# Expert weights of a mixture-of-experts kernel: which rows a partition takes

## The chip, the cores and the metric

The kernel runs on one core of a Trainium2 chip. Its time is the device time of one execution, in microseconds (us); it is given as the median of several runs. Beside the timed runs, one execution was recorded by the hardware profiler; its trace is what the views below are taken from.

## What is computed

One layer of a diffusion backbone over 128 context tokens and 256 latent tokens (T = 384), width D = 2048, in float32. The first half (modulation, input projection, attention and a short convolution, output projection) fills the first 700 us and is not touched by the change. The second half is a routed mixture of 16 experts with hidden width FF = 1024, of which each sees at most 48 tokens:

```
def ec_moe(h, w_router, w_gate, w_up, w_down):
    ...
    xs = jax.vmap(lambda hb, ib: hb[ib])(h, idx)
    a = jnp.einsum('becd,edf->becf', xs, w_gate)
    u = jnp.einsum('becd,edf->becf', xs, w_up)
    y = jnp.einsum('becf,efd->becd', jax.nn.silu(a) * u, w_down)
    y = y * gate[..., None].astype(y.dtype)
    ...
```

So each expert needs three matrices of 8 MiB: w_gate and w_up with 2048 rows of 1024 numbers (4 KB a row), w_down with 1024 rows of 2048 numbers (8 KB a row). All 16 experts together read 384 MiB (403 MB) of weights from HBM once.

## The kernel before

**Slots and order.** The experts are taken in eight pairs. A pair has six matrices in the order MATS: gate and up of expert 0, gate of expert 1, down of expert 0, up of expert 1, down of expert 1. Each matrix comes in four parts of 2 MiB, so a pair has 24 parts, q0 to q23: q0 to q3 gate 0, q4 to q7 up 0, q8 to q11 gate 1, q12 to q15 down 0, q16 to q19 up 1, q20 to q23 down 1. A part lies in one of the eight slots of the tile `ring`, 16 KB in each of the 128 partitions (the list ORDER says which part goes to which slot). SyncE (SP) issues one DMA per part (`expert_load`, L345 to L356): it waits on `moe_used` until the part that had the slot eight parts ago has been used, and then issues. The first eight loads wait for tiles of the first half that lie in the same memory. TensorE (PE) waits on `moe_landed` of the slot, uses it, and raises `moe_used`.

**Rows and partitions.** A gate or up part is 512 rows. Partition p takes the rows p, 128+p, 256+p and 384+p, that is, 4 runs of 4 KB. A down part is a block of 512 of the 2048 columns of all 1024 rows: partition p takes that block of the rows k*128+p, that is, 8 runs of 2 KB.

**Matmuls.** The tokens of an expert are the 64 stationary columns. `up_or_gate` makes, for each of the 4 row groups, two matmuls of 512 columns, the two halves of FF, into the upper and the lower 64 rows of one PSUM bank. `down` (L740) makes, for each of 8 row groups, two matmuls of 256 columns, again one in each half of the array; each part gives 512 of the output columns. Every float32 matmul stands in the trace as two instructions, so a part of gate or up is 16 of them and a part of down 32. All of them are recorded at one line, L428.

**Around them.** ScalarE makes silu of the gate bank into `act` (L1053), VectorE multiplies it by the up bank (L1462), TensorE transposes it (`turn_act`, L753), VectorE copies it to `actT` (L1474), and then down can start. After q7 TensorE also adds the pair before into the result: 16 `send_chunk` matmuls, which VectorE drains. Ahead of q20 it gathers the tokens of the next pair (`gather`, 48 matmuls, that is 96 instructions) from `h2_rows`, which ScalarE wrote once, ahead of the experts, with 12 copies out of PSUM (`rows_copy_out`). In the last pair, the parts of down 1 go to banks of their own, and each is followed by its share of the result (`send_last`, `turn_result`), which SP stores.

The modulation weights `in_w_ada` of the first half are loaded by SP, too, in 16 DMAs of 2 MiB into slots of the same `ring`. There, each partition takes one run of 16 KB out of one row of 48 KB:

```
sp.dma_start(ring[:, n, :], ada_rows[bass.ds(i * 4 * P + n * P, P), 0:SLOT]).then_inc(w_landed[n], 16)
```

Of the kernel before, what the change touches and what calls it, by code (L numbers as in the profile page):

```python
# [16 lines left out]
ALU = mybir.AluOpType  # L17
ACT = mybir.ActivationFunctionType
AX_X = mybir.AxisListType.X

P = 128
D = 2048
# [3 lines left out]
NT = T // P  # L26
# [10 lines left out]
FF = D // 2  # L37
# [3 lines left out]
PAIRS = NE // 2  # L41
ES = 64
# [6 lines left out]
BLK = 512  # L49
# [36 lines left out]
def build(nc, x_prompt, x_sample, cache_k, cache_v, c, c_ctx, w_ada, b_ada, g_norm1, w_in, g_q, g_k, conv_w,  # L86
          g_attn_out, g_conv_out, w_out, g_norm2, w_router, w_gate, w_up, w_down, consts,
          y_prompt, y_sample, state_k, state_v):
    with ExitStack() as ctx:
# [220 lines left out]
        @block.sync  # L310
        def _(sp):
            for n in range(NT):
                src = x_prompt[0] if n == 0 else x_sample[0, (n - 1) * P:n * P, :]
                sp.dma_start(x_rows[:, n, :], src).then_inc(x_in[n], 16)

            sp.wait_ge(small_in, 16 * 11)

            for n in range(4):
                sp.dma_start(ring[:, n, :], ada_rows[n * P:(n + 1) * P, 0:SLOT]).then_inc(w_landed[n], 16)
            with sp.Fori(1, N_ADA1 // 4) as i:  # L320
                for n in range(4):
                    sp.wait_ge(w_used, 4 * i + (n - 3))
                    sp.dma_start(ring[:, n, :], ada_rows[bass.ds(i * 4 * P + n * P, P), 0:SLOT]).then_inc(w_landed[n], 16)

            def unit_load(u, src, half, col, more=0):

                if u >= RAW:
                    sp.wait_ge(lo_ready, more + (u - RAW + 1))
                elif u == RAW - 1:
                    sp.wait_ge(w_used, N_ADA1 - 2)  # L330
                elif u == 0:
                    sp.wait_ge(w_used, N_ADA1 - 3)
                sp.dma_start(raw_unit(u).rearrange("p (k n) -> p k n", n=UC), src[:, 8 * half:8 * half + 8, bass.ds(col, UC)])\
                    .then_inc(raw_landed[u % RAW], 16)

            for u in range(U_QKV):
                unit_load(u, in_rows, u % 2, u // 2 * UC)
            with sp.Fori(0, D_CONV // UC) as i:
                for j in range(6):
                    unit_load(U_QKV + j, in_rows, j % 2, i * UC + (o_u, o_c, o_b)[j // 2], 6 * i)  # L340
            for j, (b, half) in enumerate(OUT_UNITS):
                unit_load(U_QKV + U_CONV + j, out_rows, half, b * UC)

            def expert_load(pair, q):
                what, e = MATS[q // 4]  # L345
                part, slot = q % 4, ORDER[q % RING]
                dst = ring[:, slot, :]
                if what == "d":

                    src = down_rows[bass.ds(pair * 2 * FF + e * FF, FF), part * BLK:(part + 1) * BLK].rearrange("(k p) n -> p k n", p=P)  # L350
                    dst = dst.rearrange("p (k n) -> p k n", n=BLK)
                else:
                    src = (gate_rows if what == "g" else up_rows)[bass.ds(pair * 2 * D + e * D + part * 512, 512), :]\
                        .rearrange("(k p) n -> p k n", p=P)
                    dst = dst.rearrange("p (k n) -> p k n", k=4)
                sp.dma_start(dst, src).then_inc(moe_landed[slot], 16)  # L356


            sp.wait_ge(unit_used, U_QKV + U_CONV)
            for q in range(RING):  # L360
                if ORDER[q] == 7:
                    sp.wait_ge(ada_free, 2 + 64)
                if ORDER[q] == 0:
                    sp.wait_ge(lo_ready, U_ALL)
                if ORDER[q] == 2:
                    sp.wait_ge(unit_used, U_ALL)
                if ORDER[q] == 3:
                    sp.wait_ge(logits_done, 1)
                if ORDER[q] == 1:
                    sp.wait_ge(routed, 1)  # L370
                    sp.wait_ge(h2_pool, len(H2_POOL))
                expert_load(0, q)
            with sp.Fori(0, PAIRS - 1) as i:
                for j in range(PER_PAIR):
                    sp.wait_ge(moe_used, PER_PAIR * i + (j + 1))
                    expert_load(i + (j + RING) // PER_PAIR, (j + RING) % PER_PAIR)
            for j in range(PER_PAIR - RING):
                sp.wait_ge(moe_used, PER_PAIR * (PAIRS - 1) + j + 1)
                expert_load(PAIRS - 1, j + RING)


            for q in range(4):
                cols = slice(q * BLK, (q + 1) * BLK)
                sp.wait_ge(last_out, NT * (q + 1))
                sp.dma_start(y_prompt[0, :, cols], y_rows[:, 0, cols]).then_inc(y_stored, 16)
                sp.dma_start(y_sample[0, :, cols].rearrange("(n p) d -> p n d", p=P), y_rows[:, 1:NT, cols]).then_inc(y_stored, 16)
            sp.wait_ge(y_stored, 16 * 8)
# [38 lines left out]
        def _(pe):  # L426
# [294 lines left out]
                for q in range(4):  # L721
                    gather_quarter(q)

            def send_chunk(k, b):

                n, o = k // 2 % 2, k // 4 * UC + k % 2 * P
                mm(bank[b][:, 0:T], y_sb[n][:, o:o + P], giveT[n], True, True).then_inc(sent, 1)


# [7 lines left out]
                                  xs[:, k, e * ES:(e + 1) * ES], ring[:, slot, off:off + BLK], k == 0, k == KC - 1)  # L737
                return last

            def down(slot, e, part, out):  # L740

                for f in range(FC):
                    rows = actT[:, (f % 4) * P + (f // 4) * ES:(f % 4) * P + (f // 4 + 1) * ES]
                    for half in range(2):
                        off = (2 * f + half) * UC
                        row = ES * (half ^ e)
                        last = mm(out[row:row + ES, :], rows, ring[:, slot, off:off + UC], f == 0, f == FC - 1)
                return last
# [6 lines left out]
                pe.wait_ge(giveT_ready, 2 * i + 2)  # L755
                pe.wait_ge(actT_ready, 2 * i + (e + 1))

            def landed(i, q):
                pe.wait_ge(moe_landed[ORDER[q % RING]], 48 * i + 16 * (q // RING + 1))

            def round_of(i, first=False, last_pair=False):
                for q in range(PER_PAIR):
# [19 lines left out]
                    if part == 0 and what == "d":  # L782
# [5 lines left out]
                        if not start:  # L788
                            pe.wait_ge(y_out, 2 * i + e)
                        turn_act(i, e)  # L790
                    landed(i, q)
                    if what != "d":
                        last = up_or_gate(slot, what, e, part)
                    elif last_pair and e == 1:
                        last = down(slot, e, part, bank[LAST_BANKS[part]][:, 0:UC])
                    else:
                        last = down(slot, e, part, bank[2 + part // 2][:, part % 2 * UC:(part % 2 + 1) * UC])
                    last.then_inc(moe_used, 1)
                    if q == 7:
                        if not first:  # L800
# [18 lines left out]
            def send_last(q):  # L819

                pe.wait_ge(y_last, q + 1)
                if q == 0:
                    pe.wait_ge(y_out, 2 * PAIRS - 1)
                for k, b in zip(chunks_of(q), [4, 5, 6, 7] if q == 0 else [7, 4, 5, 6]):
                    if q and b < 7:
                        pe.wait_ge(last_out, NT * (q - 1) + b - 3)
                    send_chunk(k, b)

            def turn_result(q):

# [16 lines left out]
        def _(act_e):  # L847
            a = act_e

            def copy(out, in_):  # L850
                return nc.scalar.activation(out, in_, ACT.Copy)  # L851
# [173 lines left out]
            def rows_copy_out(groups):  # L1025
                for g in groups:
                    a.wait_ge(rows_turned, g + 1)
                    kk = g // NT * BLK
                    copy(h2_rows[:, g % NT, kk:kk + BLK], rows_banks[g % 4][:, :]).then_inc(rows_out, 1)

            for m, k in enumerate(H2_ACT):
                a.wait_ge(h2n_ready, m + 1)
# [16 lines left out]
            def silu(i, e, first):  # L1049
                a.wait_ge(moe_used, PER_PAIR * i + (4 + 8 * e))  # L1050
                if not (first and e == 0):
                    a.wait_ge(act_turned, 2 * i + e)
                nc.scalar.activation(act, bank[0][:, :], ACT.Silu).then_inc(sil_ready, 1)  # L1053

            def rows_copy(i, e):
                a.wait_ge(moe_used, PER_PAIR * i + (16 + 8 * e))
# [39 lines left out]
        def _(v):  # L1096
# [361 lines left out]
            def round_of(i, first=False, last_pair=False):  # L1458
                for e in range(2):
                    v.wait_ge(sil_ready, 2 * i + (e + 1))  # L1460
                    v.wait_ge(moe_used, PER_PAIR * i + (8 if e == 0 else 20))
                    tt(act, bank[1][:, :], act, ALU.mult).then_inc(act_ready, 1)  # L1462
                    if e == 0:
                        if not first:
                            for k in range(KC):
                                v.wait_ge(sent, 16 * i + (k - 15))
                                add(k, 4 + k % 4)
                        if not last_pair:
                            v.wait_ge(give_turned, 2 * i + 2)
                            make(i + 1)  # L1470
                    elif not last_pair:
                        xs_copy(i + 1)
                    v.wait_ge(act_turned, 2 * i + (e + 1))
                    copy(actT, bank[4][:, :]).then_inc(actT_ready, 1)  # L1474
# [58 lines left out]
```

## Time and profile before

| | before |
|---|---|
| median of 3 runs | 1697.88 us (1697.43 to 1698.84) |
| profiled execution, span | 1694.8 us |
| TensorE matmul busy | 1496.5 us, 88% |
| VectorE, ScalarE, GpSimd busy | 27%, 16%, 3% |
| bytes moved by the DMAs | 566.10 MB, mean 334 GB/s |
| the expert stage | about 700 us to 1695 us |

The span is the profiled execution's own time from its first to its last instruction. It lies 3.1 us under the median of the timed runs, which contains what lies around the span. The busy shares are means over two stages with different limits. A matmul's end is modelled, so a busy TensorE is not one at its peak. The rates of the DMAs are given for each stretch of time in the rows below, with the TensorE clock that was granted (1.00 is the upper of its two levels, 2.4 GHz).

### The profile page before, as it was taken

Reading aid. Unit: us, or ns where it says so; the run is one execution under the profiler, and the core shown is the slowest. Engines: PE = TensorE matmul, PEld = TensorE weight load, DVE = VectorE, ACT = ScalarE, POOL = GpSimd, SP = SyncE. Lnnn points to the kernel's source line nnn. Section 1 sums busy time; section 2 is a strip of 40 time slices with the busy share of each in tenths; the row PEclk is TensorE's granted clock in tenths of the full one; section 3 lists DMA queues with packets and bytes.
Section 4 is the critical chain, followed back from the end, with each engine's and each line's share of the span. In section 5 each row is a group of like instructions: output and inputs, shape, how many; then the busy total and the mean of one; then the engine's idle time right before and its main releaser. Section 6 shows DMA issues by size and latency. Waiting matters only on the chain.

```text
span 1694.8 us, 21767 instructions
## 1 busy us (share of the span) xinstructions
PE 1496.5 (88%) x9241; PEld 975.4 (58%) x9241; DVE 454.1 (27%) x876; ACT 274.2 (16%) x412; POOL 53.9 (3%) x90
## 2 busy tenths in 40 slices
PE   4569999999999999899889789889889889889887
PEld 2138887878788998546346346346346346336334
DVE  3245542444538544300110210200200200200202
ACT  3042223223324322301000000000000000000002
POOL 0000000000001001100000000000000000000000
PEclk8879999999999999999999999999999999999999
DMA  8988787786653447799999999999999999999996
GB/s 359 427 301 299 272 284 271 252 292 211 228 183 93 132 147 269 274 399 397 409 397 398 410 398 398 410 398 398 410 398 398 409 398 399 408 398 400 407 398 236
DMA packets 205565, 566.10 MB, mean 334 GB/s; under 512 B 7804, under 2 KB 62276, under 8 KB 194884
## 3 DMA queue, kind: packets, MB, share of 16 engines
q1 hardware_dynamic: 192624, 497.04, 77.0%
q0 software_dynamic: 9216, 67.11, 11.2%
q10 hardware_dynamic: 3668, 1.12, 0.3%
q8 instruction: 44, 0.72, 0.2%
q14 instruction: 13, 0.11, 0.0%
HBM read 561.84 MB, written 3.41 MB: 334 GB/s over the span
## 4 chain that ended last, share of the span: by engine, by line
PE 56%; DMA 25%; SPq 12%; DVE 4%; issue 1%; ACT 1%; ACTq 0%; DVEq 0%; POOLq 0%
PE psum L428 54%; SPq L356 12%; DMA ring<-in_w_up 11%; DMA ring<-in_w_gate 8%; DMA ring<-in_w_ada 4%; DMA ring<-in_w_in 1%; DVE w_parts L1136 1%; DVE hid L1387 0%; DVE mix L1314 0%; DMA hid<-in_b_ada 0%; DVE ring L1124 0%; PE psum L561 0%; PE psum L753 0%; ACT w_parts L851 0%; PE psum L812 0%
## 5 line engine op out<-in xcount | busy, mean ns | idle before, releaser
L428 PE MATMUL psum<-ring,hid 128*64 128x512 f32 (+1 forms) x4096 | 683.8, 488 | 118.5 <-DMA ring<-in_w_up 82.2
L428 PEld LDWEIGHTS psum<-ring,hid 128*64 128x64 f32 x4096 | 315.2, 137 | 469.6 <-issue 276.1
L428 PE MATMUL psum<-h_parts,w_parts 128*128 128x384 f32 x1152 | 212.5, 339 | 0.0
L428 PEld LDWEIGHTS psum<-h_parts,w_parts 128*128 128x128 f32 x1152 | 199.2, 188 | 16.6 <-issue 15.9
L1462 DVE TENSOR_TENSOR hid<-psum,hid 128x512 f32<-128x512 f32 x16 | 11.1, 691 | 656.0 <-PE psum L428 656.0
L851 ACT ACTIVATE hid<-psum 128x512 f32<-128x512 f32 (+5 forms) x104 | 62.8, 623 | 724.8 <-PE psum L428 496.2
L1136 DVE TENSOR_TENSOR w_parts<-ring,w_parts 128x2048 fp32r<-128x2048 f32 x52 | 119.1, 2291 | 121.0 <-ACT w_parts L851 120.4
L428 PE MATMUL psum<-ring,early 128*32 128x512 f32 (+1 forms) x780 | 115.2, 667 | 35.1 <-DMA ring<-in_w_ada 34.9
L851 ACT ACTIVATE w_parts<-ring 128x2048 fp32r<-128x2048 f32 x52 | 99.4, 1912 | 254.3 <-PE psum L428 194.6
L428 PEld LDWEIGHTS psum<-w_parts,h_parts 128*128 128x128 f32 x864 | 107.3, 195 | 28.6 <-issue 27.7
L428 PE MATMUL psum<-w_parts,h_parts 128*128 128x256 f32 x864 | 112.3, 289 | 9.1 <-DVE h_parts L1171 9.1
L428 PE MATMUL psum<-hid 128*128 128x384 f32 (+2 forms) x320 | 100.0, 462 | 0.9 <-ACT hid L851 0.9
L428 PEld LDWEIGHTS psum<-early,mix 128*128 128x128 f32 x768 | 86.5, 192 | 8.4 <-issue 8.4
L1454 DVE SCALAR_TENSOR_TENSOR res<-psum,mod,res 128x128 f32<-128x128 f32 (+1 forms) x256 | 84.2, 408 | 21.4 <-PE psum L428 20.4
L428 PE MATMUL psum<-early,mix 128*128 128x128 f32 x768 | 88.4, 276 | 1.0 <-DVE early L1436 1.0
L428 PEld LDWEIGHTS psum<-hid 128*128 128x128 f32 x320 | 58.7, 190 | 39.0 <-issue 5.9
L428 PE MATMUL psum<-attn_parts,w_parts 128*128 128x384 f32 x384 | 69.6, 339 | 3.6 <-DVE w_parts L1136 3.6
L428 PEld LDWEIGHTS psum<-attn_parts,w_parts 128*128 128x128 f32 x384 | 68.0, 191 | 4.1 <-DVE w_parts L1136 3.8
L428 PEld LDWEIGHTS psum<-ring,early 128*32 128x32 f32 (+1 forms) x780 | 20.4, 115 | 83.8 <-DMA ring<-in_w_ada 54.3
L428 PE MATMUL psum<-conv_parts,w_parts 128*128 128x384 f32 x384 | 68.1, 335 | 0.2 <-DVE conv_parts L1268 0.2
L428 PEld LDWEIGHTS psum<-conv_parts,w_parts 128*128 128x128 f32 x384 | 66.6, 188 | 0.7 <-DVE conv_parts L1268 0.7
L399 POOL DMA_DIRECT2D ring<-in_w_ada x64 | 34.2, 535 | 451.0 <-PE psum L428 451.0
(165 smaller groups left out, 531.8 us busy)
## 6 DMA issues: line engine op xcount, KB each, us to landing
ring<-in_w_gate SPq DMA_DIRECT2D x64, 2048.0 KB, 23.4
ring<-in_w_up SPq DMA_DIRECT2D x64, 2048.0 KB, 23.5
ring<-in_w_down SPq DMA_DIRECT2D x64, 2048.0 KB, 20.4
ring<-in_w_ada POOLq DMA_DIRECT2D x64, 1024.0 KB, 5.3
ring<-in_w_in SPq DMA_DIRECT2D x36, 1024.0 KB, 5.4
ring<-in_w_ada SPq DMA_DIRECT2D x16, 2048.0 KB, 16.8
ring<-in_w_out SPq DMA_DIRECT2D x16, 1024.0 KB, 5.4
mix<-in_x_sample SPq DMA_DIRECT2D x2, 1024.0 KB, 8.8
```

The source lines that it names most:

```text
L356: sp.dma_start(dst, src).then_inc(moe_landed[slot], 16)
L399: pool.dma_start(ada_buf[j], ada_rows[bass.ds(k * P, P), m * D:(m + 1) * D]).then_inc(ada_landed[j], 16)
L428: return nc.tensor.matmul(out, lhsT, rhs, start=start, stop=stop, skip_group_check=True)
L851: return nc.scalar.activation(out, in_, ACT.Copy)
L1136: tt(w_part(u, 1), raw_unit(u), w_part(u, 0).bitcast(F32), ALU.subtract).then_inc(lo_ready, 1)
L1454: last = stt(xT[:, k, lo:hi], bank[b][:, lo:hi], mod3[:, 5 * KC + k, n:n + 1], xT[:, k, lo:hi], ALU.mult, ALU.add)
L1462: tt(act, bank[1][:, :], act, ALU.mult).then_inc(act_ready, 1)
```

## The change

The loads of gate and up take the same 512 rows, but partition p takes the four consecutive rows 4p to 4p+3: 16 KB in one piece of HBM. A part of down is no longer a block of columns. It is one half of the rows (512), and of these, for partition p, two of the four consecutive rows 4p to 4p+3, with all 2048 columns: again 16 KB in one piece, 32 KB apart from partition to partition.

Since the contraction index is now grouped otherwise, the other operand of each matmul is regrouped. For gate and up that is `h2_rows`: the 12 copies read PSUM with a step of 4 numbers. For down it is `act`: silu and the product read PSUM with a step of 4 numbers and write four runs of 128. `down` walks 2 row groups by 4 blocks of 512 columns and adds over all four parts into the whole of banks 2 and 3. So the place of a chunk in `y_sb` changes, and with it `send_chunk`.

The eight down parts of the last pair keep blocks of 512 columns (`last_down_load`, `down_block`), in runs of 2 KB, with two DMAs of 1 MiB for a part. Their order of rows is regrouped in the same way.

```diff
             def expert_load(pair, q):
                 what, e = MATS[q // 4]
                 part, slot = q % 4, ORDER[q % RING]
-                dst = ring[:, slot, :]
                 if what == "d":
-
-                    src = down_rows[bass.ds(pair * 2 * FF + e * FF, FF), part * BLK:(part + 1) * BLK].rearrange("(k p) n -> p k n", p=P)
-                    dst = dst.rearrange("p (k n) -> p k n", n=BLK)
+                    src = down_rows[bass.ds(pair * 2 * FF + e * FF + part // 2 * BLK, BLK), :]\
+                        .rearrange("(p j) n -> p j n", j=4)[:, part % 2 * 2:part % 2 * 2 + 2, :]
+                    dst = ring[:, slot, :].rearrange("p (k n) -> p k n", k=2)
                 else:
                     src = (gate_rows if what == "g" else up_rows)[bass.ds(pair * 2 * D + e * D + part * 512, 512), :]\
-                        .rearrange("(k p) n -> p k n", p=P)
-                    dst = dst.rearrange("p (k n) -> p k n", k=4)
+                        .rearrange("(p k) n -> p k n", k=4)
+                    dst = ring[:, slot, :].rearrange("p (k n) -> p k n", k=4)
                 sp.dma_start(dst, src).then_inc(moe_landed[slot], 16)
+
+            def last_down_load(q):
+
+                e, part, slot = MATS[q // 4][1], q % 4, ORDER[q % RING]
+                for half in range(2):
+                    first = (PAIRS - 1) * 2 * FF + e * FF + half * BLK
+                    src = down_rows[first:first + BLK, part * BLK:(part + 1) * BLK].rearrange("(p j) n -> p j n", j=4)
+                    dst = ring[:, slot, half * 4 * BLK:(half + 1) * 4 * BLK].rearrange("p (j n) -> p j n", j=4)
+                    sp.dma_start(dst, src).then_inc(moe_landed[slot], 16)
...
-            def down(slot, e, part, out):
+            def down(slot, e, part):
+
+                for jl in range(2):
+                    half, j = part // 2, part % 2 * 2 + jl
+                    rows = actT[:, j * P + half * ES:j * P + (half + 1) * ES]
+                    for c in range(4):
+                        row = ES * (c % 2 ^ e)
+                        off = jl * D + c * BLK
+                        last = mm(bank[2 + c // 2][row:row + ES, :], rows, ring[:, slot, off:off + BLK],
+                                  part == 0 and jl == 0, part == 3 and jl == 1)
+                return last
...
-                    copy(h2_rows[:, g % NT, kk:kk + BLK], rows_banks[g % 4][:, :]).then_inc(rows_out, 1)
+                    copy(h2_rows[:, g % NT, kk:kk + BLK].rearrange("p (a b) -> p a b", a=4),
+                         rows_banks[g % 4][:, :].rearrange("p (b a) -> p a b", a=4)).then_inc(rows_out, 1)
...
-                nc.scalar.activation(act, bank[0][:, :], ACT.Silu).then_inc(sil_ready, 1)
+                nc.scalar.activation(act.rearrange("p (a b) -> p a b", a=4), bank[0][:, :].rearrange("p (b a) -> p a b", a=4),
+                                     ACT.Silu).then_inc(sil_ready, 1)
...
-                    tt(act, bank[1][:, :], act, ALU.mult).then_inc(act_ready, 1)
+                    by_row = act.rearrange("p (a b) -> p a b", a=4)
+                    tt(by_row, bank[1][:, :].rearrange("p (b a) -> p a b", a=4), by_row, ALU.mult).then_inc(act_ready, 1)
```

## Rows read from the trace of the kernel before

**Rows 1.** The page: DMA packets, queue sizes and issues (count, KB each, us to landing).

```profile
DMA packets 205565, 566.10 MB, mean 334 GB/s; under 512 B 7804, under 2 KB 62276, under 8 KB 194884
...
ring<-in_w_gate SPq DMA_DIRECT2D x64, 2048.0 KB, 23.4
```

**Rows 2.** Windows: start:end, length, busy us per engine, PEclk, DMA share, GB/s.

```profile
1195.00:1210.00 15.00, 10.61 (x50) 3.39 (x48) 0.00 (x0) 0.60 (x1) 0.00 (x0) 1.00 1.03 410
...
1235.00:1250.00 15.00, 14.17 (x103) 8.23 (x101) 0.69 (x1) 0.60 (x1) 0.00 (x0) 1.00 1.05 387
```

**Rows 3.** The chain that ended last, one pair in steady state: start us, us, what.

```profile
936.11 1.59 PE psum L428 x7
...
1061.40 1.59 PE psum L428 x7
```

**Rows 4.** Timeline of TensorE in that pair: start, us, what, [idle before].

```profile
936.11 3.65 PE L428 MATMUL psum<-ring,hid 128*64 128x512 f32 x16 [1.42 <-DMA ring<-in_w_gate]
...
946.43 3.65 PE L428 MATMUL psum<-ring,hid 128*64 128x512 f32 x16 [1.55 <-DMA ring<-in_w_up]
951.46 3.65 PE L428 MATMUL psum<-ring,hid 128*64 128x512 f32 x16 [1.38 <-DMA ring<-in_w_up]
...
961.70 3.65 PE L428 MATMUL psum<-ring,hid 128*64 128x512 f32 x16 [1.46 <-DMA ring<-in_w_up]
965.28 10.59 PE L428 MATMUL psum<-hid 128*128 128x384 f32 x32
...
976.46 13.95 PE L428 MATMUL psum<-ring,hid 128*64 128x512 f32 x64
...
991.83 10.58 PE L428 MATMUL psum<-ring,hid 128*64 128x256 f32 x96 [0.83 <-issue]
1003.87 3.67 PE L428 MATMUL psum<-ring,hid 128*64 128x256 f32 x32 [1.46 <-DMA ring<-in_w_down]
...
1024.35 3.65 PE L428 MATMUL psum<-ring,hid 128*64 128x512 f32 x16 [1.48 <-DMA ring<-in_w_up]
1027.94 10.98 PE L428 MATMUL psum<-early,mix 128*128 128x128 f32 x96
```

**Rows 5.** Window over the w_ada loads (16 KB runs), columns as in Rows 2.

```profile
20.00:90.00 70.00, 39.56 (x235) 7.87 (x233) 20.44 (x36) 11.27 (x20) 0.00 (x0) 0.78 1.01 429
```

**Rows 6.** Timeline of TensorE there: each waits for the next w_ada slot.

```profile
56.50 1.92 PE L428 MATMUL psum<-ring,early 128*32 128x512 f32 x16 [1.50 <-DMA ring<-in_w_ada]
...
90.80 1.92 PE L428 MATMUL psum<-ring,early 128*32 128x512 f32 x16 [1.58 <-DMA ring<-in_w_ada]
```

**Rows 7.** Five-microsecond windows there, slowest and fastest.

```profile
35.00:40.00 5.00, 2.94 (x16) 0.52 (x16) 0.00 (x0) 0.00 (x0) 0.00 (x0) 0.76 0.99 419
...
75.00:80.00 5.00, 1.92 (x16) 0.42 (x16) 0.00 (x0) 0.00 (x0) 0.00 (x0) 0.99 1.03 436
```

**Rows 8.** Start of the expert stage: windows, and timelines of SP and TensorE.

```profile
710.00:715.00 5.00, 5.00 (x35) 3.26 (x36) 0.79 (x2) 0.00 (x0) 0.00 (x0) 1.00 0.92 314
...
720.00:725.00 5.00, 5.00 (x26) 1.60 (x24) 0.00 (x0) 0.20 (x1) 0.00 (x0) 1.00 1.02 411
...
703.42 16.70 SPq L356 DMA_DIRECT2D ring<-in_w_gate  x4
...
814.78 3.65 PE L428 MATMUL psum<-ring,hid 128*64 128x512 f32 x16 [0.94 <-DMA ring<-in_w_gate]
```

**Rows 9.** End of the kernel, timeline of TensorE in the last pair.

```profile
1650.92 3.65 PE L428 MATMUL psum<-ring,hid 128*64 128x512 f32 x16 [1.47 <-DMA ring<-in_w_up]
1655.53 0.63 PE L753 MATMUL psum<-ident,hid 128*128 128x128 f32 x4 [0.95 <-DVE hid L1462]
```

**Rows 10.** Timelines of VectorE and ScalarE: operations that read PSUM.

```profile
678.60 0.34 DVE L1398 TENSOR_REDUCE ring<-psum 128x48 f32<-128x192 f32 x1
...
690.15 1.57 ACT L851 ACTIVATE mix<-psum 128x512 f32<-128x512 f32 x3 [0.88 <-PE psum L440]
```

**Rows 11.** Window over x_sample's load (8 KB runs, 8 KB apart), columns as in Rows 2.

```profile
5.00:10.00 5.00, 0.00 (x0) 0.00 (x0) 0.00 (x0) 1.28 (x1) 0.00 (x0) 1.00 1.02 418
```

More of the change, by code:

```diff
@@ L378, in _ @@
                 sp.wait_ge(moe_used, PER_PAIR * (PAIRS - 1) + j + 1)
-                expert_load(PAIRS - 1, j + RING)
+                if MATS[(j + RING) // 4][0] == "d":
+                    last_down_load(j + RING)
+                else:
+                    expert_load(PAIRS - 1, j + RING)
             for q in range(4):
@@ L722, in gather, with send_chunk @@
                     gather_quarter(q)
-            def send_chunk(k, b):
-                n, o = k // 2 % 2, k // 4 * UC + k % 2 * P
+            def send_chunk(k, b, by_block=False):
+                n, o = (k // 2 % 2, k // 4 * UC + k % 2 * P) if by_block else (k // 4 % 2, k // 8 * BLK + k % 4 * P)
                 mm(bank[b][:, 0:T], y_sb[n][:, o:o + P], giveT[n], True, True).then_inc(sent, 1)
@@ L738, in up_or_gate, with down_block @@
                 return last
-            def down(slot, e, part, out):
+            def down(slot, e, part):
[8 more added lines that the diff above has]
+                return last
+            def down_block(slot, e, part, out):
                 for f in range(FC):
@@ L756, in turn_act, with landed @@
                 pe.wait_ge(actT_ready, 2 * i + (e + 1))
-            def landed(i, q):
-                pe.wait_ge(moe_landed[ORDER[q % RING]], 48 * i + 16 * (q // RING + 1))
+            def landed(i, q, more=0):
+                pe.wait_ge(moe_landed[ORDER[q % RING]], 48 * i + 16 * (q // RING + 1 + more))
             def round_of(i, first=False, last_pair=False):
@@ L790, in round_of @@
                         turn_act(i, e)
-                    landed(i, q)
+                    landed(i, q, e + 1 if last_pair and what == "d" else 0)
                     if what != "d":
@@ L794, in round_of @@
                     elif last_pair and e == 1:
-                        last = down(slot, e, part, bank[LAST_BANKS[part]][:, 0:UC])
+                        last = down_block(slot, e, part, bank[LAST_BANKS[part]][:, 0:UC])
+                    elif last_pair:
+                        last = down_block(slot, e, part, bank[2 + part // 2][:, part % 2 * UC:(part % 2 + 1) * UC])
                     else:
-                        last = down(slot, e, part, bank[2 + part // 2][:, part % 2 * UC:(part % 2 + 1) * UC])
+                        last = down(slot, e, part)
                     last.then_inc(moe_used, 1)
@@ L826, in send_last @@
                         pe.wait_ge(last_out, NT * (q - 1) + b - 3)
-                    send_chunk(k, b)
+                    send_chunk(k, b, by_block=True)
             def turn_result(q):
```

## The prediction

> **What bounds the kernel now.** The first view is the table of windows, for the DMAs' rate and the clock. In the expert stage, the DMA share is above 1 (1.03 and 1.05) and the clock is at its upper level [rows 2]. The rate has two values only: 410 GB/s while gate and up parts land, 387 GB/s while down parts land [rows 2]. The second view is the chain of waits: the same point of two successive pairs lies at 936.11 and 1061.40 us, a period of 125.29 us [rows 3]. The third is TensorE's timeline in that pair. Where it waits, it waits for a DMA, and the waited parts start every 5.12 us: (961.70 − 951.46) / 2 [rows 4]. Between the starts of q7 (961.70) and q15 (1003.87, the first to wait again) lie 8 parts in 42.17 us, four gate and four down, so a down part takes (42.17 − 4 × 5.12) / 4 = 5.42 us [rows 4]. Both agree with the rates (2.097 MB / 5.12 us = 410 GB/s, 2.097 / 5.42 = 387) and with the period: 16 × 5.12 + 8 × 5.42 = 125.3 us. So this stage is a stream of DMAs without a hole, and TensorE's 88% is no bound. TensorE waits for a part 11 times in a pair (q2 to q7 and q15 to q19), 1.38 to 1.55 us each, 16.1 us in all; its own work in a pair is 125.3 − 16.1 = 109.2 us [rows 3, 4].
>
> The stream starts with q8 of the first pair, issued at 703.42 us. The windows show holes up to 720 us, while TensorE has yet to free slots, and none afterwards [rows 8]. It decides up to q19 of the last pair, whose use starts at 1650.92 [rows 9]. From q8 to there are 180 parts: 120 of gate and up, 60 of down. 120 × 5.12 + 60 × 5.42 = 939.6 us of the 947.5 us from 703.4 to 1650.9; the rest is the first landing and the holes.
>
> **The price of a row.** Each contiguous run is one packet: there are 205565 − 62276 packets of 2 KB or more, of which 194884 − 62276 = 132608 are under 8 KB [rows 1], and the code makes 128 × 512 of 4 KB plus 64 × 1024 of 2 KB, 131072. The packets of 8 KB and more are 10681; the code makes 16 × 128 of 16 KB and 8576 of 8 KB, 10624. So a 16 KB run travels whole. What a part in 16 KB runs takes is shown by w_ada: the same queue, the same tile, the same 2 MiB, one run of 16 KB per partition. TensorE, which waits for each of them, starts at 56.50 and, seven slots later, at 90.80: 4.90 us a slot [rows 6], 428 GB/s, and the window over 70 us says 429 [rows 5]. The three lengths lie on one line. Per DMA engine (16 of them), a part is 8, 32 or 64 packets; 32 − 8 more cost 5.12 − 4.90 = 0.22 us, and 64 − 32 more cost 0.30 us: 9.2 and 9.4 ns a packet.
>
> **Part by part.**
> - Gate and up, 4 runs of 4 KB become one of 16 KB: 120 parts × (5.12 − 4.90) = 26.4 us less.
> - Down, 8 runs of 2 KB become one of 16 KB, except in the last pair: of the 60 parts in the stream 56 change, × (5.42 − 4.90) = 29.1 us less. The 4 of down 0 in the last pair keep 2 KB runs and 5.42 us; their second DMA adds an issue on SP, whose queue has then nothing else to serve. At nothing, with a bound of 0 to +1 us.
> - Bound of the rate: the w_ada windows lie between 419 and 436 GB/s [rows 7], 5.00 and 4.81 us a part. That gives 120 × 0.12 + 56 × 0.42 = 37.9 us less, or 120 × 0.31 + 56 × 0.61 = 71.4 us less. I take 4.90, since it is the mean over seven slots in a row.
> - Does TensorE keep up? The new period is 24 × 4.90 = 117.6 us, against 109.2 us of work. The new `down` streams as many columns: 8 matmuls of 512 instead of 16 of 256. A dense part of 512 columns takes 13.95 / 4 = 3.49 us and one of 256 columns 10.58 / 3 = 3.53 us [rows 4]. So at nothing, −0.3 to +0.2 us a pair, and under cover of the stream. The ring covers the bursts: after q7, TensorE spends 3.6 us on q7 and 11.2 us (965.28 to 976.46) on other work; that is 3.0 parts of 4.90 us, and 3 of 8 slots fill up, so the stream does not stop. It catches up by 4.90 − 3.49 = 1.4 us a part instead of 1.6 to 1.9, and so waits again one or two parts later than now. This is the stage where "what is late next" is asked: still the DMA.
> - In the first pair TensorE works without a wait for data up to 814 us [rows 8], since eight parts were there at the start. There a faster stream meets a full ring earlier. I add nothing, with a bound of +3 us (holes and the first landing together are 947.5 − 939.6 = 7.9 us now).
> - The 12 copies to `h2_rows` read PSUM with a step of 4. No ScalarE operation of the trace has such a read. On VectorE the reduction of 192 numbers with a step of 16 takes 0.34 us, 1.8 ns a number, fixed cost included [rows 10]. For ScalarE's copies the bound is from 0 (0.52 us each, as now [rows 10]) to twice the time, +6.3 us for 12; the end of the stage before runs through VectorE and they lie beside it for the most part. At nothing; nothing speaks for a gain.
> - Silu and product with the same step, twice a pair: inside a pair 8.4 us of waiting covers them (117.6 − 109.2). At the end the product stands between q19 and the transposes (1655.53, 0.95 us after TensorE stopped [rows 9]): 0 to +0.7 us, taken as 0.
> - The tail from q19's start to the end is 1694.8 − 1650.9 = 43.9 us, made of TensorE work over the last down parts with old runs and old columns. It moves as a whole.
>
> Sum: 26.4 + 29.1 = 55.5 us. Against the profiled execution, 1694.8 − 55.5 = 1639.3 us of span; the timed median lies 3.1 us above the span, so **1642.4 us**, a gain of 3.3%.
>
> **The rule that speaks against it.** The runs of one matrix now start 16 KB apart from partition to partition (gate and up) or 32 KB (down), powers of two; w_ada's start 48 KB apart. The one row with a power of two and long runs is x_sample, 8 KB apart, 418 GB/s over a window that holds small loads too [rows 11]: it speaks against a loss. The Trainium skill, page "DMA: Bandwidth & Descriptors", section "Latency and other measured facts", says that tiles of 128 partitions with 16 KiB rows lose rate at large power-of-two row pitches: 207 GB/s at 512 KiB against 214 in full, and 103 at 4 MiB. No run here shows such a pitch. By that page a pitch of 16 or 32 KB would cost nothing, and the sum stays.
>
> **Rivals.**
> - *The address pattern slows HBM.* Sixteen engines read 64 KB (gate, up) or 128 KB (down) apart in step. Break-even is 125.3 / 24 = 5.22 us a part, 402 GB/s. If all parts fell to the slowest rate of this stage, 387 GB/s or 5.42 us, gate and up would lose 120 × 0.30 = 36 us and down gain nothing: 1734 us. Against it stands that the whole 2 MiB of a gate part is read in either order, and that down before (8 KB apart) lies on the line of packet costs. 7%.
> - *The pieces stay apart.* If the four rows of gate and up still travel as four runs and only down's rows get longer (two runs of 8 KB, 16 packets an engine, 4.90 + 8 × 0.0093 = 4.97 us), the gain is 56 × 0.45 = 25 us: 1672.7 us. For it: both sides of the DMA are still written with three dimensions, and no load of the trace has consecutive rows. Against it: the run is contiguous on both sides. 10%.
> - *TensorE becomes the bound.* If the halves of the array no longer worked side by side in the new `down`, its 8 parts would take twice 3.5 us, 28 us more: 137 us a pair, 12 us over now, and some 88 us in 7.3 pairs: 1785 us. It decides from 16.1 / 8 = 2.0 us more per down part. The new loop alternates rows 0 and 64 as gate does. 2%.
> - *Faster, but held by the start* (full ring, copies, product): 1642.4 + 3 + 6.3 + 0.7 = 1652 us; part of the forecast's own range. With the slow end of the rate, 1660 + 10 = 1670.
> - *No change within 0.2%*: 3%.
>
> **How the numbers follow.** 78% for the forecast with its own range: 1626.5 (436 GB/s) to 1670. 10% for 1672.7. The range for 8 in 10 is taken from 1626 to 1673, which leaves out the slower cases and the edges. A measurement of this kernel tells about 0.2% (3.4 us) from no change. Faster: 0.78 + 0.10 = 0.88; same 0.03; slower 0.07 + 0.02 = 0.09.
>
> **What would show it.** Right, if the windows of the stage show one rate near 428 GB/s, with no difference between gate and down; if the period of a pair is near 117.6 us; if the packets fall from 205565 by 128 × 384 (gate, up) + 56 × 896 (down) = 99328, to about 106,000; if TensorE's waits for DMAs in a pair shrink from 16 to about 8 us, and a dense down part still takes 3.5 us in 16 instructions; and if the tail is still 44 us. A rate of 410 with unchanged packets of gate is the second rival. A rate under 402 is the first. A TensorE that waits for nothing and a DMA share under 1 is the third.

## The result and the profile after

The changed kernel takes 1640.39 us (median of 4 runs, 1639.11 to 1642.69), against 1697.66 us (median of 4 runs, 1696.77 to 1698.84) for the kernel before. The ratio is 0.9662, with a 95% interval of 0.9649 to 0.9676: 57 us or 3.4% less. The forecast was 1642.4 us, and the gain that it worked out was 55.5 us.

The page of the profiled execution, its first line, its second part for PEclk, DMA and rate (40 slices of 41 us), and the packets:

```profile
span 1639.7 us, 19983 instructions
...
PEclk8779999999999999899999999999999999999999
DMA  8978878786663435689999999999999999999996
GB/s 355 428 299 299 300 265 282 243 293 225 222 227 95 127 123 230 253 343 428 428 427 428 428 428 429 428 428 428 428 428 428 428 428 428 428 428 428 421 406 236
DMA packets 106363, 566.07 MB, mean 345 GB/s; under 512 B 7932, under 2 KB 62404, under 8 KB 72132
```

From the 19th slice on, the rate is 428 GB/s; the two levels of 410 and 387 [rows 2] are gone, until the last pair's down parts bring the older runs back (421 and 406). The same bytes move in 106363 packets instead of 205565 [rows 1]. Of the packets from 2 to under 8 KB, 9728 (72132 − 62404) are left of 132608.

The chain of waits of the changed kernel, at the same point of two successive pairs (start us, us, what). It answers to [rows 3]:

```profile
947.75 14.17 PE psum L440 x48
...
1065.21 14.17 PE psum L440 x48
```

The period is 117.46 us instead of 125.29. TensorE's timeline in that pair answers to [rows 4]:

```profile
947.75 3.65 PE L440 MATMUL psum<-ring,hid 128*64 128x512 f32 x16 [1.24 <-DMA ring<-in_w_up]
951.33 10.59 PE L440 MATMUL psum<-hid 128*128 128x384 f32 x32
...
962.51 13.96 PE L440 MATMUL psum<-ring,hid 128*64 128x512 f32 x64
...
977.88 17.58 PE L440 MATMUL psum<-ring,hid 128*64 128x512 f32 x80 [0.83 <-issue]
996.69 3.65 PE L440 MATMUL psum<-ring,hid 128*64 128x512 f32 x16 [1.24 <-DMA ring<-in_w_up]
1001.59 3.65 PE L440 MATMUL psum<-ring,hid 128*64 128x512 f32 x16 [1.25 <-DMA ring<-in_w_up]
1006.49 3.65 PE L440 MATMUL psum<-ring,hid 128*64 128x512 f32 x16 [1.24 <-DMA ring<-in_w_up]
...
1022.48 27.69 PE L440 MATMUL psum<-ring,hid 128*64 128x512 f32 x128 [0.99 <-issue]
1050.63 3.65 PE L440 MATMUL psum<-ring,hid 128*64 128x512 f32 x16 [0.46 <-DMA ring<-in_w_up]
```

Read it in this order. The waited parts start every 4.90 us: (1006.49 − 996.69) / 2. TensorE waits for data again at q17 instead of q15 (the group of 80 instructions is the four parts of down 0 and q16), and after the gather at q4 instead of q2 or q3 (the 128 instructions from 1022.48 are the four parts of down 1 and q0 to q3, 3.46 us each). Of TensorE's waiting for DMAs in a pair, 7.8 us are left, in 7 waits. Before, it was 14.7 us in 10 waits; the prediction's 16.1 us in 11 counts one too many, as the part on the prediction shows. It is still the DMA that is late.

### The profile page after: what moved, and what is told of

It is laid out like the page before. It is cut to its first block, busy times and chain, and to the rows that moved or that the text cites. A ratio compares the mean times of both kernels' runs of the same rounds, so it can differ in the third digit from the quotient of the medians.

```text
span 1639.7 us, 19983 instructions
## 1 busy us (share of the span) xinstructions
PE 1493.5 (91%) x8345; PEld 908.4 (55%) x8345; DVE 454.4 (28%) x876; ACT 274.3 (17%) x412; POOL 54.0 (3%) x90
## 2 busy tenths in 40 slices
DMA packets 106363, 566.07 MB, mean 345 GB/s; under 512 B 7932, under 2 KB 62404, under 8 KB 72132
## 4 chain that ended last, share of the span: by engine, by line
PE 64%; DMA 30%; DVE 4%; issue 1%; ACT 1%; ACTq 0%; DVEq 0%; SPq 0%
PE psum L440 62%; DMA ring<-in_w_up 25%; DMA ring<-in_w_ada 3%; DMA ring<-in_w_in 1%; DVE w_parts L1164 1%; DVE hid L1415 1%; DVE mix L1342 0%; DMA hid<-in_b_ada 0%; DVE ring L1152 0%; PE psum L452 0%; PE psum L573 0%; ACT w_parts L877 0%; PE psum L838 0%; PE psum L860 0%; PE psum L777 0%
## 5 line engine op out<-in xcount | busy, mean ns | idle before, releaser
L440 PEld LDWEIGHTS psum<-ring,hid 128*64 128x64 f32 x3200 | 246.3, 137 | 482.4 <-issue 384.7
L440 PE MATMUL psum<-ring,early 128*32 128x512 f32 (+1 forms) x780 | 116.7, 676 | 34.1 <-DMA ring<-in_w_ada 34.0
```

What stands on the lines that cost most here:

```text
L440: return nc.tensor.matmul(out, lhsT, rhs, start=start, stop=stop, skip_group_check=True)
```

## Experiments

The theory that all of them test: a part of 2 MiB costs 4.82 us plus about 9.3 ns for each packet that one of the 16 engines moves, and nothing else of the change counts in the stream. The rivals are that the order of the addresses brings the gain (or costs something), and that the new `down` on TensorE does.

### One half of the change at a time

gu_only has only the new loads of gate and up, with the copies to `h2_rows`:

```diff
-                        .rearrange("(k p) n -> p k n", p=P)
+                        .rearrange("(p k) n -> p k n", k=4)
```

> Only gate and up take consecutive rows (with the regrouped copies to h2_rows); down keeps its blocks of 512 columns in 2 KB runs. Theory (a part of 2 MiB takes 4.82 us plus about 9.3 ns for each packet of an engine, and nothing else of the change counts): 120 parts x 0.22 us = 26.4 us less than before, 1671.3 us; period of a pair 16 x 4.90 + 8 x 5.42 = 121.8 us; two rates in the windows, 428 and 387 GB/s. Rival (the gain comes from the new down on TensorE: half as many matmuls and weight loads): nothing gained here, 1697 us.

Measured: 1670.56 us, ratio 0.9833 (0.9816 to 0.9849); expected 1671.3. Its period is 1076.82 − 955.13 = 121.7 us:

```profile
955.13 14.17 PE psum L428 x48
1076.82 14.17 PE psum L428 x48
```

down_only is the other half: the changed kernel with this one line and the copies put back.

> Only down changes (16 KB runs, two row groups by four blocks of 512 columns); gate and up keep four runs of 4 KB. Theory: 56 parts x 0.52 us = 29.1 us less than before, 1668.6 us; period 16 x 5.12 + 8 x 4.90 = 121.1 us; rates 410 and 428 GB/s. The two halves of the change add up to the whole (55.5). Rival (down's new form on TensorE brings the gain): the whole gain of 57 us is here, 1640 us.

Measured: 1667.11 us, ratio 0.9815 (0.9799 to 0.9831); expected 1668.6. The period is 1072.78 − 951.73 = 121.05 us. On their chip the kernel before took 1698.29 us. The halves gain 27.7 and 31.2 us, 58.9 together, and the whole gained 57. So they add up within the spread of the runs (under 3 us within each kernel), and neither half is the carrier of the whole. With gu_only falls the rival that puts the whole gain on TensorE, since TensorE's down has its old form there. It doesn't yet say that down's own 31 us come from the packets, because down_only changes both the loads and the matmuls; the next three runs do.

### The same addresses in smaller pieces

Here the changed kernel keeps its row order, its slots and its matmuls. Only the longest piece that one descriptor may carry is limited (4096, 8192 and 2048 bytes):

```diff
-                sp.dma_start(dst, src).then_inc(moe_landed[slot], 16)
+                sp.dma_start(dst, src, max_dma_last_dim=4096).then_inc(moe_landed[slot], 16)
```

> The changed kernel with one thing undone: the loads of gate, up and down still take consecutive rows into the same places, but every run is cut into descriptors of 4 KB. Theory (number of packets alone): 32 packets per engine and part, 5.12 us; gate and up gain nothing against before, down gains 56 x 0.30 = 16.8 us: 1680.9 us, period 122.9 us, one rate of 410 GB/s, packets up by about 71,000 against the changed kernel. Rival (the order of addresses is what counts: each partition reads consecutive rows, HBM likes it): stays at 1640 us, 117.5 us a pair.

> The same with descriptors of 8 KB. Theory: 16 packets per engine and part, 4.82 + 16 x 0.0093 = 4.97 us; 176 parts x 0.074 = 13 us over the changed kernel, 1653.5 us, period 119.3 us, 422 GB/s. Rival (address order): 1640 us.

> The changed kernel with every run of the expert loads cut into descriptors of 2 KB. Theory (number of packets alone): 64 packets per engine and part, 5.42 us for all; gate and up lose 120 x 0.30 = 36 us against before, down gains nothing: about 1734 us, period 130.1 us, 387 GB/s throughout. Rival (address order counts): 1640 us.

Measured: cap4 1681.53 us (ratio 0.9897, 0.988 to 0.9913), cap8 1654.70 us (0.9739, 0.9723 to 0.9755), cap2 1731.12 us in one run beside a before of 1698.2. Expected were 1680.9, 1653.5 and 1734. The packets on the page of cap4, and a window of 200 us in its steady state and in cap8's (start:end, length, busy us per engine, PEclk, DMA share, GB/s):

```profile
DMA packets 177019, 566.07 MB, mean 337 GB/s; under 512 B 7932, under 2 KB 62404, under 8 KB 166340
...
1200.00:1400.00 200.00, 176.96 (x864) 78.38 (x861) 30.58 (x80) 11.89 (x17) 0.00 (x0) 1.00 1.03 410
```

```profile
1200.00:1400.00 200.00, 182.05 (x913) 82.59 (x913) 25.46 (x64) 13.24 (x19) 0.00 (x0) 1.00 1.01 422
```

The table puts each kernel's period of a pair beside its packets per engine and part:

| kernel | run | packets | period | per part |
|---|---|---|---|---|
| run32, below | 32 KB | 4 | 116.58 | 4.858 |
| after | 16 KB | 8 | 117.46 | 4.894 |
| cap8 | 8 KB | 16 | 119.29 | 4.970 |
| cap4 | 4 KB | 32 | 122.88 | 5.120 |
| cap2 | 2 KB | 64 | 130.11 | 5.421 |

From row to row, one packet more costs 9.2, 9.5, 9.3 and 9.4 ns, worked out from the periods. (The first of these is not packets alone: run32 also issues half as many DMAs.) cap4 and before have the same time for gate and up, 5.12 us, though the order of the rows is another. So the address order earns nothing: all of the gain is the number of packets. And cap2 is slower than before by 33 us, with the same matmuls as the changed kernel. Its down parts, in TensorE's new form and the new row order but in pieces of 2 KB, take 5.42 us as before; so down's gain isn't TensorE's either.

### A pitch of 512 KB

The loads of `expert_load` were moved so that a partition's run of 16 KB lies 512 KB after its neighbour's. The kernel so multiplies with rows of other experts.

```diff
-                    src = (gate_rows if what == "g" else up_rows)[bass.ds(pair * 2 * D + e * D + part * 512, 512), :]\
-                        .rearrange("(p k) n -> p k n", k=4)
+                    src = (gate_rows if what == "g" else up_rows).rearrange("(g p k) n -> g p k n", g=2, k=128)[e, :, bass.ds(pair * 16 + part * 4, 4), :]
```

> Loads of the same size in runs of 16 KB, but from partition to partition the run moves on by 512 KB instead of 16 or 32 KB, in gate, up and down (the kernel so multiplies with rows of other experts; every byte is still read once, except in the last pair's down). Theory (packets alone): 4.90 us a part, 1640 us, period 117.5 us. Rival (power-of-two pitches cost rate, the case that the prediction held against the change): the Trainium skill, page DMA: Bandwidth & Descriptors, section Latency and other measured facts, gives 207 of 214 GB/s at this pitch; in its proportion a part would take 4.90 / 0.967 = 5.07 us, 176 parts 30 us more, 1670 us.

Measured: 1641.40 us in one run, with this window (the changed kernel has 429 GB/s in it, too):

```profile
1200.00:1400.00 200.00, 184.83 (x930) 82.95 (x928) 19.30 (x46) 13.20 (x17) 0.00 (x0) 1.00 1.01 429
```

So the rival that held power-of-two pitches against the change has no ground at 512 KB, let alone at 16 or 32 KB. The Trainium skill's rule (page "DMA: Bandwidth & Descriptors", section "Latency and other measured facts") gives 207 GB/s for copies between HBM tensors at this pitch, against 214 in full; this load into SBUF shows no such loss. The rule has no figure for a pitch under 512 KiB. That 16 and 32 KB would cost nothing the prediction inferred from the trend of its figures; the 428 GB/s of the changed kernel bear it out. Pitches of 2 MiB and more were not tried.

### Half of the bytes

After the first eight parts, only the first half of each slot is filled:

```diff
+                    if not full:
+                        src, dst = src[:, 0:2, :], dst[:, 0:2, :]
```

> Each expert load after the first eight brings only the first 8 KB of a partition's 16 KB (half of the weights are left out; TensorE multiplies whatever lies in the slot). All else is as in the changed kernel. It measures TensorE's own work in a pair. Theory: a DMA takes about 2.5 us, less than the 3.49 us of a part on TensorE, so TensorE is the bound at 109.2 us a pair; q7 of pair 1 at about 829 us as now, six pairs on 1484, q19 at 1539, plus 43.4 of tail: 1582 us of span, about 1584 us. Rival (TensorE's own work is near the 117.5 us of the stream, and the change is already bound by it): close to 1640 us.

Measured: 1572.98 us in one run, span 1571.3; expected 1582 of span. TensorE's timeline, the sends after q7 in two successive pairs and the work between:

```profile
937.69 10.59 PE L444 MATMUL psum<-hid 128*128 128x384 f32 x32
...
1004.26 41.42 PE L444 MATMUL psum<-ring,hid 128*64 128x512 f32 x192 [0.99 <-issue]
1045.61 10.59 PE L444 MATMUL psum<-hid 128*128 128x384 f32 x32
```

TensorE waits for no DMA, and a pair takes 1045.61 − 937.69 = 107.92 us. This is TensorE's own floor with the new `down`. The changed kernel lies 9.5 us a pair above it, the kernel before 17.4. The expectation of 109.2 was 1.3 us too high, which is 7.8 us of the miss in six pairs; another 2.5 us is that this execution started on the experts at 698.53 instead of 701.05 us. How the 109.2 came about is told in the part on the prediction.

### A step further: runs of 32 KB

If only packets count, longer runs must gain again. run32 fills two neighbouring slots with one DMA. For that ORDER is [4, 5, 6, 7, 2, 3, 0, 1], the first eight loads are issued in another order, and the rows of gate and up are grouped by eight. The loop of the loads:

```diff
-                for j in range(PER_PAIR):
-                    sp.wait_ge(moe_used, PER_PAIR * i + (j + 1))
-                    expert_load(i + (j + RING) // PER_PAIR, (j + RING) % PER_PAIR)
+                for j in range(0, PER_PAIR, 2):
+                    sp.wait_ge(moe_used, PER_PAIR * i + (j + 2))
+                    expert_load_two(i + (j + RING) // PER_PAIR, (j + RING) % PER_PAIR)
```

> A step further: in the stream, two neighbouring slots are filled by one DMA of 4 MiB in runs of 32 KB (gate and up in groups of eight rows); the first eight parts and the last sixteen stay single, in runs of 16 KB or 2 KB. Theory: 4 packets per engine and 2 MiB, 4.86 us; 160 parts x 0.037 = 5.9 us less than the changed kernel: 1634.5 us, period 116.7 us. Rival (grain: slots come free and land in pairs, the ring holds only four of them, and it runs dry in the bursts of other work on TensorE): 1640 us or more, with windows under 420 GB/s and longer waits of TensorE.

Measured: 1641.15 us, ratio 0.966 (0.9644 to 0.9676): nothing gained over the changed kernel. Yet the stream does run faster, as the theory has it. Window of run32:

```profile
1200.00:1400.00 200.00, 184.89 (x930) 84.05 (x930) 21.97 (x53) 14.07 (x19) 0.00 (x0) 0.99 1.00 432
```

432 GB/s, and a period of 1299.40 − 1182.82 = 116.58 us between the starts of q6, where 116.7 was expected. (The expectation counted 160 parts in pairs. The loop loads 84 pairs, that is 168 parts, for which 6.2 us would be gained instead of 5.9.) So the gain of the stream was given away elsewhere. SP's timeline shows one place, the first load of the stream (start, us, what):

```profile
711.25 10.21 SPq L369 DMA_DIRECT2D ring<-in_w_gate  x2
```

It is issued at 711.25 us, since two slots must be free. In the changed kernel the same view has:

```profile
704.92 16.65 SPq L356 DMA_DIRECT2D ring<-in_w_gate  x4
```

A second place is TensorE. Its waits are now 2.54 us long, and after some of them the same 32 instructions take longer; two lines of its timeline in run32, and then windows over the first of them and the 8 us before it:

```profile
833.07 8.78 PE L453 MATMUL psum<-ring,hid 128*64 128x512 f32 x32 [2.54 <-DMA ring<-in_w_up]
...
1182.82 7.09 PE L453 MATMUL psum<-ring,hid 128*64 128x512 f32 x32 [2.54 <-DMA ring<-in_w_up]
```

```profile
825.00:830.00 5.00, 5.00 (x26) 1.90 (x22) 0.00 (x0) 0.00 (x0) 0.00 (x0) 1.00 1.02 436
830.00:833.00 3.00, 0.53 (x4) 0.00 (x0) 0.00 (x0) 0.00 (x0) 0.00 (x0) 1.00 1.03 437
833.00:835.00 2.00, 1.93 (x6) 0.69 (x8) 0.00 (x0) 0.00 (x0) 0.00 (x0) 0.59 1.10 475
```

The granted clock is 0.59 in the 2 us after the wait (between its two levels of 1.00 and half), and these 32 instructions take 8.78 instead of 7.09 us. Two explanations were so open. run32b tests the first: q8 to q11 of the first pair are loaded singly (TensorE's waits on the slots follow), all else is run32.

```diff
-            with sp.Fori(0, PAIRS - 1) as i:
+            for j in range(4):
+                sp.wait_ge(moe_used, j + 1)
+                expert_load(0, j + RING)
+            for j in range(4, PER_PAIR, 2):
+                sp.wait_ge(moe_used, j + 2)
+                expert_load_two((j + RING) // PER_PAIR, (j + RING) % PER_PAIR)
+            with sp.Fori(1, PAIRS - 1) as i:
...
```

> run32 with one thing changed: q8 to q11 of the first pair are loaded singly, as soon as one slot is free; the pairs of slots (4 MiB, 32 KB runs) start after them. In run32 the stream itself ran at 116.6 us a pair, but its first load was issued at 711.25 us instead of 704.92. Theory (what run32 lost is this start): 6.3 us come back, less 4 x 0.037: 1641.2 - 6.2 = 1635 us. Rival (run32 lost it at the end and to TensorE's clock, which fell to about half after waits of 2.5 us): at most 2 us come back, 1639 to 1641 us.

> The changed kernel itself, beside run32b on the same chip: 1640.4 us, ratio to before 0.966.

Measured, both on one chip: run32b 1635.32 us (1634.09 to 1635.61), ratio 0.9633 (0.962 to 0.9646); the changed kernel 1640.01 us (1639.01 to 1640.13), ratio 0.966 (0.9647 to 0.9673); before 1697.60. Against run32, 5.8 us came back of 6.2 expected, or 5.2 us if each is set against the kernel before on its own chip. The rival had at most 2 us, so the start by two slots is a cause of run32's loss.

How much of the loss it is by itself, the runs don't show. The two profiled executions lie 7.5 us apart (1640.1 and 1632.6 us). The first issue is at 703.44 instead of 711.25 us, but the start of q6 in the next pair, where TensorE waits for the stream, moves only from 833.07 to 828.85, by 4.2 us. And 1.6 us of these are the clock in the gather ahead of the experts (7.22 us in run32, 5.60 in run32b; see "A thing that it did not see"). The remaining 3.3 us arise in the last pair: 1.6 before q19, which isn't explained, and 1.7 in the first part of down 1. There run32's granted clock is 0.73 from 1600 to 1603 us. That part in run32, and then in run32b:

```profile
1601.16 5.36 PE L453 MATMUL psum<-ring,hid 128*64 128x256 f32 x32 [0.83 <-DVE hid L1522]
...
1595.38 3.67 PE L459 MATMUL psum<-ring,hid 128*64 128x256 f32 x32 [0.83 <-DVE hid L1528]
```

So in these two traces the start itself is worth about 2.6 us. The slow groups inside the stream cost nothing visible: one of 8.78 us stands in run32b, too (at 1295 us), and the period is 116.6 us in both.

Against the changed kernel run32b gains 4.7 us, where the packets of its 164 paired parts would give 6.0; the profiled executions lie 5.9 us apart (1638.5 and 1632.6), so the runs don't tell the two numbers apart. run32b is the fastest kernel of this study; its range and the changed kernel's do not touch.

## Why the prediction was right

**The bound.** It took the stage as one stream of DMAs. The floor of TensorE, measured by itself (107.9 us a pair), and the windows (one rate of 428 GB/s) bear that out.

One reading in it is wrong: TensorE's own work of 109.2 us a pair. The prediction took 11 waits (16.1 us) off the period of 125.29 us between 936.11 and 1061.40 us. But the first of them, before q2, ends at 936.11, ahead of that period, and at its end the first part that waits visibly is q3:

```profile
1066.51 3.65 PE L428 MATMUL psum<-ring,hid 128*64 128x512 f32 x16 [1.46 <-DMA ring<-in_w_gate]
```

From the sends at 965.28 us on, every pair has ten waits, 14.7 us in all. That leaves 110.6 us, 2.7 above the measured floor. Nearly all of this can be named. Groups of 4, 6 and 8 dense parts stand with 13.95, 20.82 and 27.69 us, that is, 3.44 us a part and 0.21 us once for the group. So each of the ten waited parts, which stand with 3.65 us, hides 0.21 us of idle time (the ends of matmuls are modelled). Another 0.4 us is q2, whose data land at 1061.35 us, just after TensorE could have begun (an estimate from the same 3.44 us). So it is luck that 109.2 lies near 107.9: a wait too many and these hidden bits nearly cancel. The sum doesn't use the number. It served only to say that TensorE keeps up, and there the true margin is wider than the forecast one (9.5 us a pair against 8.4).

**The price of a part.** Taken from the w_ada loads, 4.90 us; measured 4.894. The line of 9.2 and 9.4 ns a packet, drawn through three points, holds for five, from 4 to 64 packets. This is the step on which the sum rested, and cap8, cap4 and cap2 were foretold by it within 3 us.

**The terms.** 26.4 us for gate and up: 27.7 measured. 29.1 us for down: 31.2. They are 1.3 and 2.1 us under the measured ones; the 95% intervals of the two ratios are 2.8 us wide to either side. With the measured 4.894 us a part in place of 4.90 the sum is 27.1 + 29.5 = 56.6 us, against 57.3 between the medians. The span came out at 1639.7 us where 1639.3 was forecast, with 1.5 us of late start in it (below). The last step, 3.1 us from span to median, was too large: here it is 0.7 us. In every later run the profiled execution's time lies 1.6 to 1.8 us above its span, so the profiled execution of the kernel before was probably about 1.4 us under its median. q19 of the last pair starts at 1596.34 us instead of 1650.92 [rows 9]: 54.6 us, while TensorE's first expert part started 1.5 us later than before (701.05 against 699.55).

**What it took at nothing.** The copies that read PSUM with a step of 4 take as long as before; this is the line of ScalarE's timeline in the changed kernel that answers to [rows 10]:

```profile
690.36 1.57 ACT L877 ACTIVATE mix<-psum 128x512 f32<-128x512 f32 x3 [0.88 <-PE psum L452]
```

So the bound of +6.3 us was far too careful. Silu (0.60 us) and the product (0.69 us) take as long as before, too; and at the end TensorE's transposes start 4.61 us after q19 in both (1600.95 − 1596.34; 1655.53 − 1650.92 [rows 9]). The new `down` takes 3.46 us a dense part, as said. The full ring costs nothing visible: the windows of 5 us from 720 us on stay at 416 to 436 GB/s. The tail is 43.4 us instead of 43.9.

**A thing that it did not see.** The 1.5 us of late start is TensorE's clock. In the profiled execution of the changed kernel the gather of 48 instructions takes 7.22 us, and the granted clock is 0.64 between 693 and 696 us; before it took 5.60 at 1.00. In a second profiled execution of the same changed kernel it takes 5.60 again:

```profile
693.43 5.60 PE L440 MATMUL psum<-early,mix 128*128 128x128 f32 x48 [0.98 <-DVE early L1464]
```

So it belongs to the execution and not to the change. Dips of this kind stand in other profiled executions, too (the gather takes 7.22 us in run32 and pitch512, and the first part of down 1 in the last pair takes 5.36 instead of 3.67 us in gu_only, cap4 and run32). Each is worth 1.6 to 1.7 us, so two spans that differ by that much differ by nothing of the kernels.

**The rivals.** "The pieces stay apart" is refuted by the packets; cap8 and cap4 show what it would have cost (14 us for pieces of 8 KB and 41 us for 4 KB everywhere). "The address pattern slows HBM" is refuted by pitch512, also at a far larger pitch. "TensorE becomes the bound" did not come: a dense part of the new down takes 3.46 us and not twice 3.5, so the two halves of the array still work side by side. It would need 9.5 us more work in a pair.

## What to carry to other kernels

Where a stage is one unbroken stream of DMAs, count the packets that each engine moves: here, each cost 9.4 ns on top of the bytes, in both row orders and at pitches of 16, 32 and 512 KB. So let each partition take consecutive rows, and regroup the other operand where it is copied anyway; a read of PSUM with a step of 4 was free on both engines. Longer pieces also make coarser grain: look at when the first load of the stream can be issued, and keep small pieces there (with them, the kernel of 32 KB runs was 5 to 6 us faster).

## What the runs showed of the hardware

- The cost of a packet is constant from 2 KB to 32 KB: 9.2 to 9.5 ns on an engine. What is left of a DMA of 2 MiB when the line is drawn to no packets at all is 4.82 us (435 GB/s); this is worked out from the table, and no run had such a rate over a pair.
- A run of 32 KB travels as one packet: run32 has 12097 packets fewer than the changed kernel; 84 DMAs that take the place of 168 save 84 × 128 = 10752 of data, and 1344 = 84 × 16 under 512 B went with them.
- Loads with neighbouring partitions 16, 32 and 512 KB apart ran at the same 428 to 429 GB/s.
- After waits of 2.5 us between otherwise dense work, TensorE's granted clock fell to 0.59 in a window of 2 us in some cases (833 us) and stayed at 1.00 in others (1183 us), in one and the same execution. What decides this was not found.
